# A hand-planned fp32 transformer kernel on one core: filling around a gate, a broadcast by matmul, and three moved subtractions

## Time and profile before

| what | value |
|---|---|
| median of 3 runs | 2151.11 us (2150.1 to 2152.01) |
| the profiled execution: its time | 2151.45 us |
| the profiled execution: its span | 2149.7 us |
| PE busy | 2100.8 us (98%) |
| DVE busy | 1417.2 us (66%) |
| ACT busy | 1051.5 us (49%) |
| DMA engines, mean busy share | 50% |

### The profile page before, as it was taken

The page is one execution under the profiler, slowest core; times in us unless marked ns, Lnnn a source line. Parts: engine busy times, 40 slices in busy tenths (PEclk is TensorE's granted clock), DMA queues, the critical chain, the costliest instruction groups (busy, mean ns, idle before and its releaser), DMA issues.

```text
span 2149.7 us, 27722 instructions
## 1 busy us (share of the span) xinstructions
PE 2100.8 (98%) x11555; PEld 1802.3 (84%) x11555; DVE 1417.2 (66%) x1802; ACT 1051.5 (49%) x1520; POOL 109.4 (5%) x121
## 2 busy tenths in 40 slices
PE   7999999999899999999999999999999999999998
PEld 6989888988887888787888888888888878888887
DVE  5657876757777766665775666576666666755665
ACT  5444545544544544544544445454545454454543
POOL 0100200100011100000000000000100000000000
PEclk9999999999999999999999999999999999999999
DMA  8353235353234765445455465565645445554552
GB/s 280 121 197 118 83 134 183 120 195 128 76 127 158 242 207 170 151 149 162 171 181 179 139 207 196 185 216 181 210 150 181 139 161 172 194 170 154 185 188 98
DMA packets 193125, 357.76 MB, mean 166 GB/s; under 512 B 8364, under 2 KB 85352, under 8 KB 193000
## 3 DMA queue, kind: packets, MB, share of 16 engines
q1 hardware_dynamic: 190120, 345.51, 47.9%
q0 software_dynamic: 2880, 10.49, 1.5%
HBM read 354.92 MB, written 1.05 MB: 166 GB/s over the span
## 4 chain that ended last, share of the span: by engine, by line
PE 72%; DVE 8%; ACT 2%; issue 1%; POOL 0%; DMA 0%; DVEq 0%; ACTq 0%
PE bank L1976 13%; PE bank L1980 13%; PE bank L1986 13%; PE bank L2018 12%; PE bank L2022 6%; DVE raw_r L2485 3%; PE bank L2040 2%; PE bank L2031 2%; PE bank L2057 1%; PE bank L2000 1%; PE bank L2006 1%; PE bank L2003 1%; PE bank L2160 1%; PE bank L2048 1%; PE bank L2243 1%; PE bank L2078 1%
## 5 line engine op out<-in xcount | busy, mean ns | idle before, releaser
L2485 DVE TENSOR_TENSOR raw_r<-raw,high 128x2048 fp32r<-128x2048 f32 x304 | 686.8, 2273 | 75.9 <-ACT high L2269 74.8
L2269 ACT ACTIVATE high<-raw 128x2048 fp32r<-128x2048 f32 x304 | 575.2, 1896 | 228.8 <-PE bank L1986 178.3
L1976 PE MATMUL bank<-high,units_r 128*128 128x512 f32 (+1 forms) x1576 | 629.2, 399 | 4.9 <-ACT units_r L2286 4.9
L1980 PE MATMUL bank<-high,units_r 128*128 128x512 f32 (+1 forms) x1576 | 615.7, 391 | 2.2 <-DVE units_r L2509 1.3
L1986 PE MATMUL bank<-raw_r,units_r 128*128 128x512 f32 (+1 forms) x1576 | 422.9, 389 | 3.4 <-DVE raw_r L2485 3.4
L1976 PEld LDWEIGHTS bank<-high,units_r 128*128 128x128 f32 x1576 | 296.9, 188 | 66.4 <-issue 7.6
L1986 PEld LDWEIGHTS bank<-raw_r,units_r 128*128 128x128 f32 x1576 | 295.3, 188 | 66.7 <-DVE raw_r L2485 4.9
L1980 PEld LDWEIGHTS bank<-high,units_r 128*128 128x128 f32 x1576 | 297.0, 188 | 62.4 <-DVE units_r L2509 2.6
L2018 PE MATMUL bank<-units_r,high 128*128 128x512 f32 x1152 | 288.2, 392 | 0.4 <-DVE units L2841 0.4
L2018 PEld LDWEIGHTS bank<-units_r,high 128*128 128x128 f32 x1152 | 208.4, 189 | 38.7 <-issue 0.6
L2022 PEld LDWEIGHTS bank<-units_r,raw_r 128*128 128x128 f32 x1152 | 157.2, 190 | 11.2
(11 more groups left out here) (258 smaller groups left out, 2216.4 us busy)
## 6 DMA issues: line engine op xcount, KB each, us to landing
raw<-in_ffn_w_dram SPq DMA_DIRECT2D x132, 1024.0 KB, 5.1
raw<-in_w_in_dram SPq DMA_DIRECT2D x108, 1024.0 KB, 5.1
raw<-in_w_out_dram SPq DMA_DIRECT2D x24, 1024.0 KB, 4.9
raw<-in_cross_wkv_dram SPq DMA_DIRECT2D x16, 1024.0 KB, 5.0
raw<-in_w_branch_dram SPq DMA_DIRECT2D x12, 1024.0 KB, 4.9
raw<-in_cross_wq_dram SPq DMA_DIRECT2D x8, 1024.0 KB, 5.0
raw<-in_cross_wo_dram SPq DMA_DIRECT2D x8, 1024.0 KB, 4.9
raw<-in_w_in_dram SPq DMA_DIRECT2D x4, 832.0 KB, 4.4
```

The lines of the kernel that those rows point to most:

```text
L1976: pe.matmul(o, h.high(k0 + k)[:, span], p.hi[k][:, cols], start=start and k == 0, stop=False, skip_group_check=True)
L1980: pe.matmul(o, h.low(k0 + k)[:, span], p.hi[k][:, cols], start=False, stop=False, skip_group_check=True)
L2269: done = act.activation(high, raw, ACT.Copy)
L2485: done = dve.tensor_tensor(low, raw, high.bitcast(F32), ALU.subtract)
```

## The change

1. **The start.** The gain row is loaded once (4 KB, SP, ahead of x) and spread over the partitions by two matmuls with a row of ones into two banks; `norm_scale` reads the gain there. The transfer on POOL's queue is gone for this seam. x comes in halves, each with a semaphore, ahead of the identity. `begin` of the first seam lists: turn of the first rows, split of their first half, high and low part of piece 0, split of their second half, the second rows' norm, and then the products with both halves of the rows for each pair of pieces, with `turn_row(1)` after the very first `tok`.
2. **Filling.** A `"rest"` in `spread` ends the filling, but no longer forgives the missing work. `recurrence` gives one main step before it begins, and `hgrn_heads` gives one after the first `level_mul`.
3. **The gate.** Each part is followed by a rest, `bounded` is cut in three parts, and `decay` and `log_key` are parts of their own.
4. **Low parts.** `tail` no longer ends with `low_next`; `turn(1)` calls it between `norm_squares` and `norm_mean`. In `mixing` one `low_next` comes ahead of the last `branch(1)`.
5. **Tables.** `tables` starts with 12 empty steps.
6. `later` keeps its list in order of time.

```diff
@@ spread
             if step == "rest":
-                ahead = 0
+                break
@@ later
-        self.lag.append((self.work + us * 2400, part))
+        at = self.work + us * 2400
+        i = sum(due <= at for due, _ in self.lag)
+        self.lag.insert(i, (at, part))
@@ turn_pairs
             h.made(t, q, name)
+            if between and q == 0:
+                between()
@@ Seam
-        if norm:
+        self.gain = gain
+        if norm and not gain:
             plan.do("gpre", name=name, src=gain_rows.pop(0), used=plan.gpre_used)
...
     def turn(self, t):
-        for _ in self.steps(t):
-            pass
+        for i, _ in enumerate(self.steps(t)):
+            if t and i == 2:
+                self.plan.low_next()
@@ tail
-    plan.low_next()
     plan.hold = True
     put(*toks[-1])
@@ begin
     if seam.yb is None:
-        plan.split_next(True)
-        steps = seam.steps(1)
-        next(steps)
+        def first_piece():
+            plan.split_next(True)
+            plan.low_next()
+
+        seam.turn_row(0, first_piece)
+        for _ in seam.steps(1):
+            pass
+        plan.lead = LEAD
+        for i, (name, w, banks) in enumerate(make_jobs()):
+            for t in range(2):
+                for pi, (k0, p) in enumerate(w):
+                    if i == t == 0 and pi == len(w) - 1:
+                        seam.turn_row(1)
+                        plan.hold = False
+                    plan.tok(name, p, t, [banks[t]], seam.h, k0, pi == 0, pi == len(w) - 1)
+                    yield
+        return seam.h
+    if seam.h is None:
         seam.turn_row(0)
...
@@ make_plan
+    do("load_gain", src=gain_rows.pop(0))
+    do("load_x", t=0, dst=plan.xt[0].ap)
     do("load_ident")
-    do("load_x", t=0, dst=plan.xt[0].ap)
...
     def tables():
+        for _ in range(12):
+            yield 0
@@ hgrn_qf
+            parts = [(softplus, 0), (softplus, 1), (forget, 0), (forget, 1)]
+            parts += [(bounded, phase) for phase in range(3)] if l else []
+            parts += [(decay,), (log_key,)]
+
+            def gate_f():
+                yield "rest"
+                for part, *how in parts:
+                    part(*how)
+                    yield "rest"
@@ hgrn_heads
             level_exp(0)
             level_from(1)
             yield
+            level_mul(0)
+            yield
             old = 0
             for li, lev in enumerate(levels):
-                if li == 0:
-                    level_mul(0)
@@ tensor_program
+    def gain_row(banks, **_):
+        hold.wait_ge(*at(("ones",)))
+        hold.wait_ge(*at(("gain_in",)))
+        for i, b in enumerate(banks):
+            pe.matmul(b.ap, m.gT[0:1, 0:P], m.gpre[0:1, i * 512:i * 512 + 512], start=True, stop=True,
+                      skip_group_check=True).then_inc(*mark(s.turned, ("gain_row", i)))
+        hold.wait_ge(*at(("ident",)))
@@ sync_program
+        for i in range(2):
+            sl = slice(i * 512, i * 512 + 512)
+            sp.dma_start(dst[:, sl], A["x"][0, t * P:(t + 1) * P, sl]).then_inc(
+                *mark(s.x[2 * t + i], ("x_in", t, i), by=16))
```

More of the change, by code:

```diff
@@ L170, in __init__ @@
         self.pstep = sem("s_pstep")
[L172 removed]
+        self.x = [sem(f"s_x{i}") for i in range(4)]
+        self.gain = sem("s_gain")
         self.const = sem("s_const")
@@ L719, in turn_row @@
         tmp, name = self.row[t], f"{self.name}.h{t}"
-        self.plan.turn_pairs(name, tmp.ap, [[("row", f"{self.name}.n{t}", i)] for i in range(2)], self.h, t)
+        self.plan.turn_pairs(name, tmp.ap, [[("row", f"{self.name}.n{t}", i)] for i in range(2)], self.h, t,
+                             between=between)
         self.plan.U.give(tmp, ("turnp", name, 1))
@@ L741, in steps @@
         if self.norm:
-            for self.row[t] in plan.norm(nn, x, plan.x_made[t], ("gpre", self.name), plan.m.gpre[:, :]):
+            for self.row[t] in plan.norm(nn, x, plan.x_made[t], *(self.gain or ([("gpre", self.name)] * 2, plan.gpre))):
                 yield
@@ L791, in begin @@
     if seam.yb is None:
-        plan.split_next(True)
-        steps = seam.steps(1)
-        next(steps)
-        seam.turn_row(0)
-        for _ in steps:
-            pass
-        plan.hold = False
-        plan.pump()
-    else:
-        if seam.h is None:
-            seam.turn_row(0)
-        seam.turn(1)
+        def first_piece():
[15 more added lines that the diff above has]
+    if seam.h is None:
+        seam.turn_row(0)
+    seam.turn(1)
     plan.lead = LEAD
-    jobs = make_jobs()
-    yield from plan.mm_halves(jobs, seam.h, lambda: seam.turn_row(1))
+    yield from plan.mm_halves(list(make_jobs()), seam.h, lambda: seam.turn_row(1))
     return seam.h
@@ L898, in first_layer @@
         N = f"a{l}"
+        made = []
         def jobs():
-            return [(f"{N}.kv{br}", plan.weight(w_in, 0, 8, c0, 512), [B.take(), B.take()])
-                    for br, c0 in enumerate((5632, 6144))]
-        made = []
-        h = yield from begin(plan, seam, lambda: made.extend(jobs()) or made)
+            for br, c0 in enumerate((5632, 6144)):
+                made.append((f"{N}.kv{br}", plan.weight(w_in, 0, 8, c0, 512), [B.take(), B.take()]))
+                yield made[-1]
+        h = yield from begin(plan, seam, jobs)
         if l == 0:
+            for b in g_banks:
+                B.give(b, ("row", "in.n1", 1))
             setup()
@@ L1914, in drive @@
                 return e.value
-    seam = Seam(plan, "in", gain_rows)
+    g_banks = [B.take(), B.take()]
+    do("gain_row", banks=g_banks)
+    seam = Seam(plan, "in", gain_rows, gain=([("gain_row", i) for i in range(2)], [b.ap for b in g_banks]))
     seam.turn(0)
```

81 lines of the change are left out of this document (45 added, 36 removed).

## The result

The changed kernel takes 2127.71 us (median of 4 runs, 2125.75 to 2129.75) where the kernel before took 2151.56 on the same chip (4 runs, 2150.1 to 2152.78). The ratio is 0.989, with a 95% interval of 0.9872 to 0.9907. The profiled execution took 2127.4 us, with a span of 2125.6; it was 2149.7 before.

A forecast was written before the change was run, and what follows sets the result against it. PE bounds the kernel, busy 2100.8 of 2149.7 us; only its waits and half-clock stretches can shrink. Terms -3.6 - 2.7 - 9.2 - 4.6 + 0.3 + 0 + 1.0 = -18.8 give 2132.3 us median; range 2122 to 2145, own range 2128 to 2138.

The forecast's parts named there:

- The start, -3.6: Kernel start: new order of work and lighter loads bring the first product to 11.2 us; 3.6 us saved, bounds 1.6 to 5.5.
- 0.5 MB of gain transfer is gone from ahead of it, which is 1.5 us: Kernel start: without the gain transfer ahead of it, piece 0 comes 1.5 us earlier, at 336 GB/s.
- at most 0.7: Kernel start: the most that x in halves and the scaling are worth, in us.
- The recurrence's begin, -2.7: First-stack layers: added main steps end waits for the copy of q and the first level's product; 2.7 us saved, at worst 1.3.
- The gate, -9.2: Attention's gate scaling, both first-stack layers: denser filling shortens waits and removes slow clock; 9.2 us saved, bounds 0 to 17.9.
- filling missing later, +1.0: End of each first-stack layer: eight main steps bare instead of six; 1.0 us lost, at worst 5.1.
- the 2.9 of slow clock gone: Layer 0, behind the gate's 3.55 us wait: the half-clock stretch, costing 2.9 us, disappears.
- `forget`, `decay` and `log_key` are done before the critical scores: Layer 0's gate: these parts finish ahead of the critical scores, leaving a wait of 1 us in place of 3.55.
- the waits only move: Rival, gate: each group of waits is replaced by its like, with its slow clock; gate term 0, 2141.5 us; chance 0.25.
- The seams, -4.6: Seams between stages: moved low parts and tables shorten waits for normed rows; 4.6 us saved, bounds 2.5 to 6.0.
- the tables' +0.3: Tables' later place under ffn1's products: one late exp costs 0.3 us, at most 1.5.
- Mixing, 0: Mixing's end: the first low part comes in time, but PE waits for the second instead; 0 us, at best 2.1 saved.

The follow-up runs named there:

- the ten: Ten profiled traces sharing the changed kernel's start: its own and nine variants; the first product began between 11.01 and 12.31 us.
- steps_back: Changed kernel without the two added main steps of the recurrence; ratio to the kernel before 0.9913.
- middle_back: Changed kernel with forgiving rests, the gate's last parts in one step and no added main steps, all as before; ratio to the kernel before 0.995.
- gate_later: Changed kernel with one more rest at the beginning of the gate's parts, so each comes one filling step later; ratio to the kernel before 0.9905.
- rest_forgives: Changed kernel with only the filling's rest steps as before, forgiving missing work and not ending the step's filling; ratio to the kernel before 0.9919.
- mix_low_back: Changed kernel with only the low part at mixing's end put back behind the last branch; ratio to the kernel before 0.9898.
- start_order_back: Changed kernel with only the order of work at the start as before; gain row and halves of x stay new; ratio to the kernel before 0.9918.
- piece1_waits: Changed kernel with the second weight piece issued only when piece 0 has landed; ratio to the kernel before 0.9901.
- gain_whole: Changed kernel with the first gain read again as 0.5 MB for all partitions, behind the first rows of x; ratio to the kernel before 0.991.
- rest_softplus: Changed kernel in which, of the gate's parts, only the two softplus end their step's filling; ratio to the kernel before 0.9894.
- parts_back: Changed kernel with only the gate's last parts (bounded, decay, log_key) put back into one filling step; ratio to the kernel before 0.9897.
- seam_low_back: Changed kernel with only the low part at the seams put back ahead of the second rows' norm; ratio to the kernel before 0.9924.
- tables_early: Changed kernel without the twelve empty steps ahead of lambda and the rope tables; ratio to the kernel before 0.9912.

## Why the prediction came out right, and which terms were off

The mechanisms of the seams, the recurrence's begin and mixing were right. That the total came this near is in part luck, for its misses cancel. By an estimate with the clock's usual share (2.4 us in place of the 6.8 of these two traces) the gain is about 20 us, near the 18.8 of the sum, but made otherwise: the seams gave 3.6 more than forecast and the bare steps cost 1.0 less, the clock gave 2.2 less and the start 1.2 less.

By the forecast's own list of signs: the waits of the first level's product went, of those for the copy of q one stayed (1.0); the line of L2101 was to be below 4 and is 4.4; one stretch at low clock was allowed and there is one; the seams' waits were to be near 1 us and are; mixing's L2010 was to wait about 1 and waits 1.28. Of the wrong signs one came true: the first product was held by its piece beyond 12 us, in this profile and in five more of the ten.

**The start, -3.6.** Measured -2.4 in the profile compared, -3.2 in the middle of ten. The order of work did what was said (low part and turn without a wait). The step that failed is the transfer: "0.5 MB of gain transfer is gone from ahead of it, which is 1.5 us". The piece landed at 9.0 to 10.4, around the old 9.80. The prediction left out that the piece is issued 0.84 us later behind four issues, and from issue to split the piece took 6.5 to 7.9 us in the ten against 8.1 before, so 0.3 to 1.6 less; why that varies by 1.3 us stays open. The forecast's 11.2 for the first product is near the best of the ten. What PE does earlier than 18 us it does at half pace, so it is worth half; that was not in the sum, and the late end of the slow pace is what made this profile's start the latest of the ten. The term's "at most 0.7" for x and the scaling was low, the first turn begins 1.1 us earlier (7.30 for 8.41), which gives nothing, as the piece comes later.

**The recurrence's begin, -2.7.** steps_back measures 3.4. The first level's waits went as said, and of those for the copy of q one of 1.0 stayed. Not foreseen was that the same steps lengthen L2213's wait by 1.4 in layer 0; what they give in the rest of both layers pays for it.

**The gate, -9.2, and filling missing later, +1.0.** With the begin the forecast for the inside of both layers is -10.9; it is -13.8 by the landmarks (5.75 + 8.09). In the forecast 7.3 of this was waits, 4.6 clock and +1.0 bare steps; measured are 7.1, 6.8 and 0. So the waits were right in sum. The slow clock was priced by the 43% of the earlier trace rows times 6.8 us, but that window begins 1 us behind the stretch (232.7 to 239.5); over 232 to 240 it is 3.4, not 2.9, and so at 560. The second long stretch was to stay and only one of 1.7 did. Both are partly luck: in middle_back the wait of 3.55 is back and the slow stretch behind it is not, so "the 2.9 of slow clock gone" with the wait was a step that the runs do not bear out. And the bare steps at the end of each layer cost nothing where +1.0 was set. Against that, layer 0's wait was to be 1 us and is 2.12: the step "`forget`, `decay` and `log_key` are done before the critical scores" failed, since two forget operations stand in front of the scaling of the earlier scores instead (1.2 us, by gate_later). The prediction's account of the old wait was half right: it named `forget`, but the exps, late as they ran behind softplus, had ended at 229.2 and held nothing, as DVE's own list put the scaling at 232.47. In layer 1 4.3 us of waits were expected and 2.30, 1.01 and 0.23 are there. The rests were rightly named as a cause (3.3 us), and the parts' moving forward was not: steps_back leaves layer 0's gate wait as it is.

The rival "the waits only move" (2141.5) had the right mechanism at one place: when gate_later moved the parts, a wait for ACT's copies came. What the change gained seems to come from more products between the parts, not from a better place for them; that is argued from rest_forgives and steps_back, not shown by a run of its own.

The table loads were priced by the trace. The trace after has again 1.28 us for one (215.22, the next operation at 216.51), and layer 1 kept its gain. By the Trainium skill's figure of 2.66 us a switch (page "ScalarE: Activation LUTs", section "What ACT_TABLE_LOAD costs") it would have been lost, by the prediction's estimate; the measurement decides against the figure here.

**The seams, -4.6, and the tables' +0.3.** By the landmarks -7.9, against -4.3; undone, the low part measures 5.5 and the tables 2.6. The mechanism was right in both. The sizes were off since only listed waits were counted: at the seam into mixing a wait of 0.56 cost 0.71, the turn's second half has its own 0.15, and a seam without a listed wait gains too. Those for which 1.7 stood (four were counted, five gain) gave 3.8. This is the largest error of the sum.

**Mixing, 0.** mix_low_back: 0.1 a layer.

So the terms of -18.8 were off by +1.2 (start), -2.9 (inside the layers) and -3.6 (seams), which makes the -24.1 of the profiles; the medians differ by 23.9. Of the -2.9, 2.2 is clock, which another pair of traces would give otherwise. The range held, and the forecast's own range just missed.

## What to carry to other kernels

Put every product's low part, table step or copy where its engine idles for something else, and count the result in landmarks of both traces, not in listed waits: five small seams gave twice their waits. Filling is counted in products, but each product brings its loads and splits to other engines' lists, so look at what the added product puts ahead of the critical operation (2.28 us of DVE here). To name the engine that holds an operation, compare the ends of all its inputs with its start: here the exps were done and DVE's own list was what counted, though a table load and a softplus stood in plain sight. Moving a block of ACT work past one consumer made the next one wait (4.59 us in layer 1 of gate_later). Near the start, read PE's pace from its matmuls and not from PEclk.

## What the hardware showed beyond the forecast

After the same wait and before the same work the granted clock fell in some executions and not in others. In eleven traces the line of L2213 waits 1.8 to 2.4 us near 147 us; behind it the clock stayed full in seven and was halved in four, for 6.8 us in three of these and 10.2 in the fourth. The wait of some 2.1 to 2.9 us near 222 us was followed by a stretch at half clock in start_order_back, rest_forgives, steps_back, piece1_waits, gain_whole and rest_softplus, and by none in the changed kernel, parts_back, seam_low_back, tables_early and mix_low_back. The wait of 3.55 at the same place was followed by 6.8 us at half clock in the kernel before and by none in middle_back. That is worth 1.7 to 5.1 us each time, more than most edits here. It goes with the spread between runs of one kernel: the changed kernel's four runs have mean clocks of 0.999, 0.998, 0.997 and 0.999, and 0.001 of 2126 us is 2.1 us; the third, 2129.75 us, is the slowest and the fourth, 2125.75, the fastest. What decides between the two outcomes stays open.
